# A kernel of two blocks: order of the last two products of a seven-product matrix multiplication

## The reference, cut to what matters

```python
h = rms_norm(x, norm_gain[l])                     # 2048 x 1024
proj = jnp.einsum('bsd,de->bse', h, w_in[l])
q, k, v, z_attn, u_ssm, z_ssm, g = jnp.split(proj, SPLITS, axis=-1)
g_attn, g_ssm = jnp.split(g + b_gate[l], N_BRANCHES, axis=-1)
...
merged = jax.nn.sigmoid(g_attn) * jnp.einsum('bsc,cd->bsd', attn, w_branch_attn[l]) \
       + jax.nn.sigmoid(g_ssm) * jnp.einsum('bsc,cd->bsd', ssm, w_branch_ssm[l])
```

## Time and profile before

| what | value |
|---|---|
| median of 3 runs | 3547.66 us (3540.14 to 3552.55) |
| the profiled execution, its own time | 3544.84 us |
| its span | 3543.1 us |
| TensorE busy | 3380.4 us, 95% |
| VectorE busy | 1811.2 us, 51% |
| ScalarE busy | 1029.2 us, 29% |
| GpSimd busy | 1147.4 us, 32% |
| line 382 on TensorE (the seven-product stage) | 1120 records, 498.1 us, first at 20.4 us, last at 579.5 us |

### The profile page before, as it was taken

How to read it: one execution, slowest core, us unless ns; L and a number is a source line. 1 busy time by engine, 2 the same in 40 slices (tenths; PEclk the granted TensorE clock), 3 DMA queues, 4 the chain that set the end, 5 groups by cost and what they waited for, 6 DMA issues and landing times.

```text
span 3543.1 us, 32439 instructions
## 1 busy us (share of the span) xinstructions
PE 3380.4 (95%) x10992; PEld 1717.4 (48%) x10992; DVE 1811.2 (51%) x4003; ACT 1029.2 (29%) x2527; POOL 1147.4 (32%) x1499
## 2 busy tenths in 40 slices
PE   7998997999999999999999999999999996999998
PEld 4443443555444644444444444555665443444443
DVE  6767773665465573326555546744453554222222
ACT  3221112222110461002234445644332222222222
POOL 3176786730000592000000001665651101443342
PEclk9999998999999999999999999999999997999999
DMA  4244438555445012223221000000102225978885
GB/s 154 97 155 146 141 138 238 168 164 158 159 163 165 25 37 107 89 89 106 73 88 36 21 12 12 1 1 1 72 24 86 92 99 209 355 196 264 256 251 135
DMA packets 133161, 423.60 MB, mean 120 GB/s; under 512 B 20661, under 2 KB 60469, under 8 KB 116830
## 3 DMA queue, kind: packets, MB, share of 16 engines
q1 hardware_dynamic: 93388, 226.42, 19.0%
q0 software_dynamic: 31392, 153.50, 13.9%
q10 hardware_dynamic: 8208, 41.53, 3.4%
HBM read 354.96 MB, written 121.62 MB: 135 GB/s over the span
## 4 chain that ended last, share of the span: by engine, by line
PE 82%; DVE 9%; ACT 3%; DMA 2%; issue 1%; POOL 1%; SPq 1%; DVEq 0%; ACTq 0%; POOLq 0%
PE pst L144 54%; PE pst L382 10%; PE pst L149 5%; DVE arena L166 4%; PE pst L2619 3%; PE pst L2714 3%; PE pst L2622 2%; PE pst L1679 1%; DMA arena<-rotd 1%; PE pst L1594 1%; POOL arena L1647 1%; ACT arena L155 1%; DVE arena L169 1%; PE pst L1151 1%; DVE arena L172 1%
## 5 line engine op out<-in xcount | busy, mean ns | idle before, releaser
L144 PE MATMUL pst<-arena 128*128 128x512 f32 (+5 forms) x5290 | 2137.8, 560 | 33.9 <-DVE arena L1184 22.5
L144 PEld LDWEIGHTS pst<-arena 128*128 128x128 f32 (+1 forms) x5290 | 970.3, 191 | 1051.1 <-issue 1010.4
L382 PE MATMUL pst<-arena 128*128 128x512 f32 x1120 | 498.1, 604 | 18.6 <-DVE arena L166 14.7
L166 DVE TENSOR_TENSOR arena<-arena 128x512 f32<-128x512 f32 (+8 forms) x897 | 450.0, 503 | 73.1 <-ACT arena L2660 19.6
L166 POOL TENSOR_TENSOR arena<-arena 128x4 f32<-128x4 f32 (+7 forms) x784 | 432.1, 551 | 81.3 <-DVE arena L2423 20.9
L382 PEld LDWEIGHTS pst<-arena 128*128 128x128 f32 x1120 | 214.5, 193 | 288.4 <-issue 257.7
L149 PE MATMUL pst<-arena 128*128 128x128 f32 x2080 | 308.8, 280 | 42.5 <-DVE arena L256 15.1
L149 PEld LDWEIGHTS pst<-arena 128*128 128x128 f32 x2080 | 242.9, 142 | 217.4 <-issue 148.5
L1647 POOL TENSOR_SCALAR arena<-arena 128x384 f32<-128x384 f32 (+1 forms) x128 | 151.5, 1202 | 443.0 <-DVE arena L1639 441.9
L155 ACT ACTIVATE arena<-pst,arena 128x128 f32<-128x128 f32 (+1 forms) x638 | 236.7, 468 | 138.3 <-PE pst L149 135.2
L2603 POOL TENSOR_SCALAR arena<-arena 128x512 f32<-128x512 f32 (+3 forms) x160 | 218.3, 1383 | 147.2 <-DVE arena L166 137.1
(11 more groups left out here) (217 smaller groups left out, 2409.3 us busy)
## 6 DMA issues: line engine op xcount, KB each, us to landing
arena<-in_w_ada SPq DMA_DIRECT2D x48, 512.0 KB, 4.8
arena<-in_w_ug ACTq DMA_DIRECT2D x18, 1024.0 KB, 6.0
sgd<-arena ACTq DMA_DIRECT2D x32, 512.0 KB, 3.4
rotd<-arena POOLq DMA_DIRECT2D x32, 512.0 KB, 4.2
arena<-rotd SPq DMA_DIRECT2D x32, 512.0 KB, 4.8
arena<-sgd SPq DMA_DIRECT2D x16, 1024.0 KB, 7.6
arena<-pwd SPq DMA_DIRECT2D x32, 416.0 KB, 5.8
arena<-in_x SPq DMA_DIRECT2D x18, 512.0 KB, 4.3
```

Of the source, the lines that this page charges most:

```text
L144: x = t.do.matmul(o, l, r, start=(i == 0), stop=(i == len(pairs) - 1))
L166: own(v, s).tensor_tensor(o, a, b, op).then_inc(*inc(s, *event))
L382: x = t.do.matmul(st_bank(q, i), left[:, k, :], right[:, k, :], start=(name in FIRST and k == 0), stop=(k == 3), skip_group_check=name != ...
```

## The change

The two calls of the last two products of a group change places in `te_st`, so that P4 stands before P3. VectorE takes C21 before C12, ScalarE gate 1 (`PAIR[1]`) before gate 0, and SyncE stores `PAIR[1]` before `PAIR[0]` for the groups of `u`. The first wait of `sp_s5_rot` is on `c12` of the last group, now the last result. No operation is added or removed; what stands between the two products, results or gates stays where it was.

```diff
--- before.py
+++ after.py
@@ -534,12 +534,12 @@
                     te_bias(t, 4 * q - 15)
                 if q > 1:
                     te_st_product(t, q, "P2")
-                te_st_product(t, q, "P3")
+                te_st_product(t, q, "P4")
                 if q in (1, 2):
                     te_norm(t, q + 1, 4, 6)
                 if q in (4, 5):
                     te_bias(t, 4 * q - 14)
-                te_st_product(t, q, "P4")
+                te_st_product(t, q, "P3")
                 if q in (1, 2):
                     te_norm(t, q + 1, 6, 8)
                 if q in (4, 5):
@@ -576,8 +576,8 @@
                 if q + 1 < SQ:
                     ve_st_sums(v, q + 1)
                 ve_side(v, 2 * q)
+                ve_st_c21(v, q)
                 ve_st_c12(v, q)
-                ve_st_c21(v, q)
                 if q == SP_ - 1:
                     ve_st_T4(v, 1)
                 ve_side(v, 2 * q + 1)
@@ -633,13 +633,13 @@
                     ac_norm_out(a, q + 1, 5)
                 if q in (4, 5):
                     ac_bias(a, 4 * q - 14)
-                ac_st_gate(a, q, 0)
+                ac_st_gate(a, q, 1)
                 if q in (1, 2):
                     ac_norm_out(a, q + 1, 6)
                     ac_norm_out(a, q + 1, 7)
                 if q in (4, 5):
                     ac_bias(a, 4 * q - 13)
-                ac_st_gate(a, q, 1)
+                ac_st_gate(a, q, 0)
                 ac_st_load(a, q)
                 if q == 2:
                     ac_bias_row(a)
@@ -674,7 +674,7 @@
             s.do.dma_start(nsk, T["sink"]).then_inc(*dma("ld_par", "nsk"))
             for q in range(2):
                 for i in range(2):
-                    sp_st_u(s, q, i)
+                    sp_st_u(s, q, 1 - i)
             s.wait_ge(*at("side_ac", "brow"))
             s.do.dma_start(bd, brow).then_inc(*dma("st_bd", "bd"))
             s.wait_ge(*at("st_bd", "bd"))
@@ -949,8 +949,8 @@
                 if q4:
                     sp_lag(s, q4 - 1)
                 if q4 in (2, 3):
+                    sp_st_u(s, SP_ + q4 - 2, 1)
                     sp_st_u(s, SP_ + q4 - 2, 0)
-                    sp_st_u(s, SP_ + q4 - 2, 1)
             sp_lag(s, 7)
 
         def sp_lag(s, q4):
@@ -1106,7 +1106,7 @@
 
         def sp_s5_rot(s, g):
             s.wait_ge(*at("s5_ve", "G", g - 2))
-            s.wait_ge(*at("st_ve", "c21", SQ - 1))
+            s.wait_ge(*at("st_ve", "c12", SQ - 1))
             rot_stored(s, g // 2)
             s.do.dma_start(RTb[g % 2].rearrange("p a b c -> p (a b c)"), rotd[g]
                            ).then_inc(*dma(f"ld_lr{g % 2}", "rot", g))
```

## The result

The changed kernel takes 3528.22 us in the median of 10 runs (3525.13 to 3531.88). The kernel before took 3546.02 us over its 10 runs (the three on record and seven more), so the ratio is 0.9955 with a 95% interval of 0.9944 to 0.9967: 0.45% faster, about 16 to 18 us, and the whole interval lies beyond 0.3%. The forecast was 7.4 us. The profiled execution took 3529.64 us with a span of 3527.9 us (before: 3544.84 and 3543.1).

The account below looks back on a forecast made before the run. TensorE, busy 95% of the span, was taken as the bound. Five waits won 4.6 us, the bias row cost 0.4 us, the clock won 3.2 us: -7.4 us, from 3547.66 to 3540.3 us, range 3532.5 to 3550 us.

Parts of the forecast that it names:

- P4 takes the place of the wait, C22 runs beside it: At five TensorE waits of P3 for C22 (groups 0, 1, 4, 8, 17): 4.6 us won together.
- the sum: Whole kernel: -4.2 us from waits and bias row, -3.2 us from the clock, -7.4 us in all.
- The bias row: Group 2: its wait for ScalarE's copy behind the longer first gate grows from 1.33 to 1.76 us, costing 0.43 us.
- The clock: Group 0: with 1.7 us of stall left, the slow stretch of 32 records goes, 3.2 us won (bounds 0 and 3.2).
- The other reading in the prediction: Group 0's clock: a 1.7 us stall could go either way, giving -4.2 us in some runs, -7.4 us in others.
- Group 17: C22 began at 517.65, so P4 can start at 517.6: 0.80 us: Wait of P3 in group 17: 0.80 us won, 3.9 us of the 4.73 us stall stays.
- so do the chains that start from them through stores: Chains starting from VectorE's long stretches move forward with TensorE, so all of the -4.2 us arrives.
- Rival E: Group 17: the slow stretch after the 1.96 us stall goes too, another 1.7 us: 3538.6 us, chance 0.05.
- Does the gain arrive at the end?: End of the stage: all of the gain was taken to arrive, -4.6 + 0.4 = -4.2 us.
- C: End of the stage: a chain not starting on TensorE swallows the gain: 3547.7 us, chance 0.17.
- D: End of the stage: an earlier weight load stretches SyncE's read issues, tables 7.7 us later: 3551.2 us, chance 0.08.
- The range: Whole kernel's time: about 3532.5 us below, from the runs' scatter under the forecast, to 3550 us above.

Follow-up runs that it names:

- e16_before_look4: The kernel before, unchanged, profiled once more (the fourth such look): 3541.33 us.
- e5_before_ba2: The kernel before with a second buffer for the matrices BAs, so VectorE's first step no longer waits for the pwd stores: 3532.82 us against 3544.78 us.
- e6_after_ba2: The changed kernel with a second buffer for the matrices BAs: 3528.13 us, ratio 0.9954 to the kernel before.
- e15_before_look3: The kernel before, unchanged, profiled once more (the third such look): 3549.79 us.
- e9_after_rot_on_pwd: The changed kernel with one wait added on GpSimd, so its ninth rotd store starts together with the pwd stores: 3536.12 us, ratio 0.9986 to the kernel before.
- e11_groups01: The kernel before with the new order of products (P4 before P3) in groups 0 and 1 alone: 3532.78 us, ratio 0.9982.
- e12_after_lag: The changed kernel with VectorE's lag step 1 moved from behind group 9's token sums to the end of group 8: 3518.16 us, ratio 0.9938 to the kernel before.
- e10_before_rot_behind: The kernel before with GpSimd's ninth rotd store issued only when the pwd stores have landed: 3541.34 us against 3539.43 us, ratio 1.0002.
- e17_behind_again: The kernel before with the ninth rotd store again held until the pwd stores have landed: 3541.17 us against 3541.91 us, ratio 0.9993.
- e4_after_again: The changed kernel once more, no edit: 3527.26 us, ratio 0.9942 to the kernel before.

## Why the prediction was right in sign and wrong in size

**What held.** "P4 takes the place of the wait, C22 runs beside it": the stalls of groups 0, 1, 4 and 8 went as the sum said, to 0.1 us in groups 0, 1 and 4; group 8 lost all of its 1.29 us instead of 0.8, because VectorE's own wait for pwd there (1.43 us) was gone too. (`e16_before_look4`, the kernel before, lacks that wait and has no stall in group 8 either; in the six profiles this stall is 0 to 1.36 us, so the one trace with 1.29 us stood for more than it could.) The bias row cost 0.47 us (1.80 - 1.33) against 0.43. The stretch up to group 15 gave 7.1 us against 6.6, and `e5_before_ba2` against `e6_after_ba2` gave 4.7 us by median and 7.4 us by span. The clock came out as taken: no slow stretch after the 1.72 us stall, in any of the nine profiles with P4 first in group 0. The window behind that stall shows a granted clock of 1.00 in the changed kernel; before it was 0.50:

```profile
54.00:56.00 2.00, 2.00 (x7) 0.80 (x6) 1.92 (x2) 0.00 (x0) 2.00 (x1) 1.00 0.00 0
```

The other reading in the prediction, that one stall can come out either way from run to run, did not show at 1.72 us. It did show between profiles of the kernel before at P2 of group 17: 2.27 and 2.30 us with a slow stretch, 2.24 us without.

The row of VectorE's wait for pwd in group 8 of the kernel before:

```profile
265.21 2.15 DVE L166 TENSOR_TENSOR arena<-arena 128x512 f32<-128x512 f32 x3 [1.43 <-DMA pwd<-arena]
```

Two things about the clock were luck. The reading that led to the term was wrong: 1.7 us is nearer to 1.96 us, with a drop, than to 1.33 us, without one. And the term of 3.2 us was on the high side: four of the six profiles of the kernel before take 15.4 to 15.7 us for those 32 records, two 17.0 and 17.1, against 14.0, so it is worth 1.4 to 3.1 us, 2.1 in the mean. That the stretch came out near 6.6 us all the same is owed to small gains that were not in the sum: the rest of group 8's stall, 0.3 us at P2 of group 4, shorter slow stretches.

**What failed.** The step "Group 17: C22 began at 517.65, so P4 can start at 517.6: 0.80 us", and behind it "so do the chains that start from them through stores". Both took the landing of the pwd stores (11.82 us) as a fixed length that moves with the stage. It was the longest piece of that chain between P7 and P3 of group 17, and I had not asked why it took 11.8 us when that store takes 7.9 in the median of its eight. The row, from the view of line 946 in the kernel before:

```profile
DMA to landing us min/median/max: 5.9/7.9/11.8
```

The trace of before had the answer beside it: GpSimd's rotd store, issued 1.93 us ahead. GpSimd starts its tables behind group 3 and then runs by its own waits, those for its stores to land among them, so its distance to VectorE's chain can change. The measured term is 7.4 us. By the chain from P7 to the end of P3 and P4, 3.7 us are the landing (11.82 to 8.11), 0.8 us the swap and 2.4 us the slow stretch behind the stall (9.53 to 7.13); the rest is small. The slow stretch on P2 (5.40 to 3.70 us) went too, but it was no part of the gain: without it P3 waits longer, as `e15_before_look3` shows. So Rival E, which priced that stretch at 1.7 us, had a stretch that costs nothing. That the landing hangs on the rotd store is shown by `e9_after_rot_on_pwd`, which brings all of it back by placing one store; `e5_before_ba2` gains the same in this stretch by taking the wait out of the kernel before.

**What else failed.** "Does the gain arrive at the end?": nothing was lost there, as forecast, and rivals C and D fell: the first table's work is 88.7 us behind the lag step, 88.8 before, and so comes 13.4 us earlier (602.62 for 615.98). But the next stage, counted at nothing, is 3.8 us shorter. I did not test that, and its cause is open. It does not hang on the wait in front of group 17: `e9_after_rot_on_pwd` and `e11_groups01` have the long wait and 955.1 and 953.0 us there. It goes along, in most profiles, with a short wait for a load of `pwd` (1.60 us at 684.91 in the kernel before): five of the six profiles of the kernel before have it and take 957.9 to 962.1 us, the sixth lacks it and takes 956.1, and the changed kernel lacks it. `e12_after_lag` lacks it too and takes 960.1 us, so it is not the whole. A part may be scatter.

**The range.** It began at 3532.5 us, 4.3 us above the measured time. It had no case in which a transfer's length changes for the better: C and D moved the transfers only to the bad side.

**What stays open.** Why the store moved behind (`e10_before_rot_behind`, `e17_behind_again`) brings its 5.8 and 7.2 us in the profiled stretch but hardly any in the median, while `e5_before_ba2` brings 12 us. A difference between them is the next stage: 958.9 and 961.7 us in the first two, 955.0 us in the third. Whether the faster runs of the kernel before have the short wait is not known; no profile caught one. So the 7.4 us of this stretch are shown in the profiles, and that placing one store costs them in the median too; that removing the collision alone wins them is not shown.

## What to carry to other kernels

A transfer that the critical chain waits for is a term like any other: before a stage is shifted, compare its length with the median of its kind, and where it is long, find what is in flight beside it and which engine issued that. If that engine runs by its own waits, a shift of a microsecond can bring the two together or apart, and the range has to hold both. And a second buffer that takes out the wait for a store (12 us here for the kernel before) does not depend on such luck.

## What the runs showed of the hardware

The distance between GpSimd's rotd store and the pwd stores took only the values 1.93, 2.72, 3.52 and 4.31 us in the kernel before, the changed one and those with a part of the change, in steps of 0.79 us (to 0.01), and was the same to 0.01 us in all six profiles of the kernel before. The chains above show the step: VectorE does its last operations at 0.77 us each, 0.02 us apart, once GpSimd is through with its table, after up to 1.7 us each beside the table's last steps, so two (499.26, 500.05) or three (490.53 to 492.11) of them lie behind GpSimd's end. So GpSimd's table ends at a fixed point of one of VectorE's operations each time; why is not shown.

The same stores of `pwd` landed in 8.1, 11.8 and 14.8 us (the last of the three), with the rotd store 2.7 us ahead, 1.9 us ahead and 0.5 us behind. The Trainium skill ("DMA: Bandwidth & Descriptors", "Issuing engines are not separate DMA queues") says that transfers started by different engines run on the same 16 DMA engines and interleave. The runs agree in that a store of GpSimd makes one of SyncE's land up to 6.7 us later (14.77 against 8.11 us), and is itself waited for 4.6 us longer (8.05 against 3.45 us).

The length of a stall alone does not decide what the clock does. Stalls of 1.72 us (nine of nine) and 2.04 us (`e4_after_again`) left TensorE at 2.4 GHz, and so did one of 3.15 us in `e10_before_rot_behind`; one of 1.96 us in the kernel before and one of 2.51 us in `e9_after_rot_on_pwd` were followed by a slow stretch. In the kernel before itself, the stall ahead of P2 of group 17 was followed by one in five profiles (1.95 to 2.30 us) and not in the sixth (2.24 us). The stall of 2.8 us in group 0 was followed by one in all eleven profiles that have it, but of 15.4 to 17.1 us for the 32 records.
